# Transposes in one group: h of the last tile and x of the next behind the first eight products of an expert step

## The reference, cut to what matters

```python
def swiglu(x, w_gate, w_up, w_down):
    return (jax.nn.silu(x @ w_gate) * (x @ w_up)) @ w_down

    def run_block(args):            # one block: up to 128 tokens of one expert
        tok, gw, e = args
        return swiglu(x[tok], w1[e], w3[e], w2[e]).astype(F32) * gw[:, None]
...
    shared = swiglu(x, ws1, ws3, ws2).astype(F32)
    return (routed + shared).astype(h.dtype).reshape(B, T, D)
```

## Time and profile before

| | us |
|---|---|
| median of 3 executions | 2640.47 |
| lowest, highest | 2636.76, 2642.72 |
| profiled execution | 2637.47 |
| its span, first to last instruction | 2635.7 |

### The profile page before, as it was taken

How to read it: one execution, slowest core, us unless ns; L and a number is a source line. 1 busy time by engine, 2 the same in 40 slices (tenths; PEclk the granted TensorE clock), 3 DMA queues, 4 the chain that set the end, 5 groups by cost and what they waited for, 6 DMA issues and landing times. The chain is left out here.

```text
span 2635.7 us, 47416 instructions
## 1 busy us (share of the span) xinstructions
PE 2461.7 (93%) x11959; PEld 2011.9 (76%) x11960; DVE 1717.1 (65%) x2741; ACT 1012.1 (38%) x1619; POOL 988.2 (37%) x1009
## 2 busy tenths in 40 slices
PE   7999999998989999889999999999999999999990
PEld 4788777776767888668888887887888888888870
DVE  4663674557345666765567768587876768778673
ACT  2321433333432222222334445354554535445442
POOL 1211016542153677741233333333333433434344
PEclk8999999999989999989999999999999999999995
DMA  7775676756766556346869979899997989979887
GB/s 295 280 284 219 233 274 243 273 210 231 282 240 236 195 188 199 126 133 167 247 169 268 282 209 304 220 301 280 286 315 193 278 256 302 292 215 307 258 239 279
DMA packets 240999, 646.32 MB, mean 245 GB/s; under 512 B 24205, under 2 KB 37841, under 8 KB 224913
## 3 DMA queue, kind: packets, MB, share of 16 engines
q1 hardware_dynamic: 190480, 463.95, 49.1%
q0 software_dynamic: 50432, 181.27, 27.5%
HBM read 467.81 MB, written 177.33 MB: 245 GB/s over the span
## 5 line engine op out<-in xcount | busy, mean ns | idle before, releaser
L2429 PE MATMUL ps_h<-shared,x_exp_t_hi 128*128 (+1 forms) x2432 | 580.0, 391 | 7.4 <-ACT x_exp_t_hi L2196 7.4
L2429 PEld LDWEIGHTS ps_h<-shared,x_exp_t_hi 128*128 128x128 f32 x2432 | 457.2, 188 | 104.5 <-issue 9.1
L2145 POOL DMA_INDIRECT sum_d<-w_shared_raw,give x136 | 236.7, 1740 | 612.1 <-DMA sum_d<-w_shared_raw,give 276.5
L1216 PE MATMUL ps_p<-shared 128*128 128x512 f32 x1632 | 392.5, 399 | 6.5 <-DVE kvqg_out L105 3.3
L1216 PEld LDWEIGHTS ps_p<-shared 128*128 128x128 f32 x1632 | 308.5, 190 | 75.9 <-DVE kvqg_out L105 4.1
L2429 PE MATMUL ps_y<-shared,h_exp_t_hi 128*128 (+1 forms) x1216 | 342.4, 404 | 19.0 <-DVE h_exp_t_lo L2267 14.7
L2429 PE MATMUL ps_h<-shared,x_exp_t_lo 128*128 (+1 forms) x1216 | 318.6, 404 | 0.0
L2247 DVE TENSOR_TENSOR shared<-w_exp,shared (+1 forms) x256 | 307.0, 1220 | 10.0 <-ACT shared L2182 4.7
L2211 ACT ACTIVATE h_exp_t_hi<-ps_ht 128x256 fp32r<-128x256 f32 x152 | 58.4, 384 | 615.5 <-PE ps_ht L2438 613.3
L2429 PEld LDWEIGHTS ps_y<-shared,h_exp_t_hi 128*128 128x128 f32 x1216 | 220.1, 190 | 62.3 <-issue 22.0
L2182 ACT ACTIVATE shared<-w_exp (+1 forms) x256 | 255.4, 1056 | 22.5 <-DMA w_exp<-in_experts 19.5
(11 more groups left out here) (296 smaller groups left out, 3601.8 us busy)
## 6 DMA issues: line engine op xcount, KB each, us to landing
w_exp<-in_experts SPq DMA_DIRECT2D x386, 512.0 KB
shared<-hx_d SPq DMA_DIRECT2D x58, 1024.0 KB, 7.1
shared<-rec_d SPq DMA_DIRECT2D x16, 1536.0 KB
shared_raw<-in_w_mod_rest POOLq DMA_DIRECT2D x16, 1024.0 KB, 5.7
rec_d<-shared_raw SPq DMA_DIRECT2D x48, 256.0 KB, 5.0
rec_d<-kvqg_out SPq DMA_DIRECT2D x48, 256.0 KB, 4.6
hx_d<-shared SPq DMA_DIRECT2D x10, 1024.0 KB, 5.8
xt<-in_xt POOLq DMA_DIRECT2D x18, 512.0 KB, 8.3
```

Source lines behind the costliest of these rows:

```text
L1216: last = pe.matmul(ps_p[:, s % 2], hx0[:, at, x, k].bitcast(F32R), wa[w][:, k, p % 2 * HD:(p % 2 + 1) * HD].bitcast(F32R), start=(m + k == ...
L2145: pool.indirect_dma_start(sum_d[:, :], bass.IndirectOffsetOnAxis(give[:, par:par + 1], 0), y[:, par], None, compute_op=ALU.add).then_inc(a ...
L2429: last = pe.matmul(out, x[:, j * P:(j + 1) * P].bitcast(F32R), w_part[:, bass.ds(w_at + j * stride, 512)].bitcast(F32R), start=(start and ...
```

## The change

In the TensorE step the two transposes of h, which stood behind sixteen of the 24 h products, and the eight transposes of x, which stood behind all 24, are both put behind the first eight. The waits inside them move along. Nothing else is changed; the order of the products among themselves stays as it is.

```diff
                 products(ps_h[:, par], x_t[0][:, par], w[0], at, KC, 512, start=True)
+                if not isinstance(k, int) or k > 0:
+                    transposes_h(k - 1, 1 - par)
+                if not isinstance(k, int) or k >= NT - 1:
+                    transposes(k + 1, 1 - par, 0 if r is None else r + par)
                 pe.wait_ge(gu_lo, (e + 1) * N_GU)
                 products(ps_h[:, par], x_t[0][:, par], w[1], at, KC, 512)
-                if not isinstance(k, int) or k > 0:
-                    transposes_h(k - 1, 1 - par)
                 pe.wait_ge(xt_lo, (k + 1) * 2)
                 products(ps_h[:, par], x_t[1][:, par], w[0], at, KC, 512, stop=True).then_inc(h_done, 1)
-                if not isinstance(k, int) or k >= NT - 1:
-                    transposes(k + 1, 1 - par, 0 if r is None else r + par)
                 if not isinstance(k, int) or k > 0:
                     down(k - 1, 1 - par)
```

## The result

| | before | after |
|---|---|---|
| median, us (13 executions each, taken in turn) | 2641.20 | 2647.58 |
| lowest, highest | 2636.76, 2643.48 | 2639.95, 2652.60 |
| profiled execution | 2637.47 | 2649.45 |
| its span | 2635.7 | 2647.6 |

The ratio is 1.0024 with an interval of 1.0014 to 1.0033: slower by 6.4 us, where 2.1 us faster was forecast. The median of 2647.58 lies 1.6 us above the upper end of the range. The two profiled executions differ by 12.0 us, more than the medians do: that of before is 3.7 us under its median, that of after 1.9 us above its own.

The account below looks back on a forecast made before the run. TensorE was taken as the only full engine in the expert stage. The terms -5.2 + 1.6 + 1.3 + 0.2 = -2.1 us gave 2638.4 us on the median of 2640.47; the 8-in-10 range was 2632 to 2646.

Parts of the forecast that it names:

- The group's price: TensorE, each step: joining two transpose groups saves one entry and exit, 0.04 us, over 137 steps 5.2 us.
- The group costs nothing: Rival: TensorE's excess belongs to the transposes themselves, so 0 in place of -5.2, 2643.6 us; chance 0.12.
- x_exp_t_hi ... Cost 0.: Next step's first h product: x copies end 1.0 us ahead in place of 1.9, 0.6 us cover left; cost 0.
- TensorE starves at the step's start.: Rival: x_exp_t_hi's 1.0 us lead is too short, 0.1 to 0.2 us per step, about 2660 us; chance 0.06.
- Down products, +1.6 by a late H.: Weight changes: h products complete (H) later in the step, VectorE's run begins 0.27 us later at six places, 1.6 us.
- gain 0: Down product waits, 12 us: earlier h transposes take none away, as VectorE has no gap; gain 0, at most 12.
- Cover of H too thin: Rival: tile h 0.87 us later delays down products at six runs and eight steps, 2649 us; chance 0.10.
- The eight steps like the earlier trace: Steps where VectorE runs gapless to h_exp_t_lo: down products just fit, cost 0, or 0.3 us each, 2.4 us.
- The third gather.: First gather after the unrolled pair: x transposes want its tile earlier, TensorE stands 1.3 us, once (0 to 3.6).
- the waits that I put at 0 for ps_x and hg: Moved waits before the x and h transposes: x_exp_t_lo frees ps_x and hg is ready early enough; cost 0.
- The clock falls.: Rival: a run of ten transposes tips TensorE to half clock, 490 us more, 3130 us; chance 0.01.

Follow-up runs that it names:

- e3: Against before: only the h transposes move behind the first eight products, x transposes stay behind all 24; ratio 0.9994.
- e13: Against after: the joined group of ten transposes stands behind sixteen h products in place of eight; ratio to before 1.0029.
- e7: e5 with VectorE's low part of the h copy put ahead of its first two weight splits; ratio to before 1.0021.
- e12: e7 with only half of each weight piece loaded from the fourth expert on, so results are not the layer's; ratio to before 0.9927.
- e1: After, with ScalarE splitting the fourth gate/up weight piece one step earlier, together with the other three; ratio to before 1.0080.
- e2: Before, with the same ScalarE edit as e1 (fourth gate/up piece split one step earlier); ratio to before 1.0079.
- e5: After, with ScalarE's fourth gate/up split last in the step before, behind h copy and down splits; ratio to before 1.0020.

## Why the prediction was wrong

Going by its steps:

- **The group's price.** Right: 0.040 us per step predicted and measured. "The group costs nothing" falls.
- **"x_exp_t_hi ... Cost 0."** Here it failed. I followed the x copies to their end and took them for the last thing that the next start needs from ScalarE. Behind them, in the same queue, stands the fourth weight split, and where the expert ahead had a single tile the start needs that too. I read ScalarE from a quiet step, where it doesn't occur, and in the earlier trace rows, a change, only up to the tanh. The sum that I should have made: copies end at S + 7.4, a split of 1.0 behind them, so S + 8.4 before the change, 0.9 ahead of the next start at S + 9.33. 0.87 later it is at S + 9.2 to 9.3 with the next start due at S + 9.29, where an input has to be 0.4 ahead: 0.3 to 0.4 us late at each such change. Measured: 0.22, 28 times. All of it but the number of changes is in rows of before. That the first eight products behind a late input run 0.12 us slower is in no row that I had read.
- **"TensorE starves at the step's start."** This rival named the place but not the reason: it costs at 31 of 136 steps, not at each. The quiet steps show x_exp_t_hi 1.0 us ahead of S to be enough. Against the rival I had also brought the queue of 64 entries that the Trainium skill states (TensorE: Matmul & The Clock Gate, Engine queue depths), and had concluded from it that a late input matters less. The trace does not bear my conclusion out for an input that comes within 0.4 us of its product, as the row at 1450.75 shows; the queue itself no run here shows.
- **Down products, +1.6 by a late H.** Mechanism right, size too large. The waits lie in six pairs, each at a run of weight changes. Idle before the down products, in the order of time:

| | first of a pair | sum | second of a pair | sum |
|---|---|---|---|---|
| before | 0.85 0.85 0.69 0.89 0.89 0.63 | 4.8 | 1.53 2.25 0.86 0.86 0.83 0.88 | 7.2 |
| after | 0.90 0.92 0.89 0.89 0.89 0.92 | 5.4 | 0.93 1.96 1.31 1.76 1.55 2.39 | 9.9 |
| e3 | 0.50 0.51 0.81 0.54 0.51 0.51 | 3.4 | 1.93 2.10 1.25 0.83 2.15 0.84 | 9.1 |
| e13 | 0.84 0.82 0.87 0.94 0.91 0.98 | 5.4 | 0.87 0.90 1.00 0.86 0.84 1.61 | 6.1 |

The first of a pair is VectorE's, as I had read it. A later H makes it 0.1 us longer, in after and e13 alike: 0.6 us in place of 1.6. h transposes alone ahead (e3) make it 0.24 shorter, so my "gain 0" was not exact either, 1.4 us, which the second ones took back. The second is 0.85 at its least, and above 1 us it is another matter, that I had missed although 1.53 and 2.25 stood in the trace of before: ScalarE waits for a load. The largest but one in after, ScalarE, VectorE and TensorE:

```profile
1801.48 1.06 ACT L2182 ACTIVATE shared<-w_exp  x1 [1.70 <-DMA w_exp<-in_experts]
1802.90 1.07 ACT L2182 ACTIVATE shared<-w_exp  x1 [0.36 <-DMA w_exp<-in_experts]
1807.67 1.06 ACT L2182 ACTIVATE shared<-w_exp  x1 [3.71 <-DMA w_exp<-in_experts]
1808.64 0.37 ACT L2211 ACTIVATE h_exp_t_hi<-ps_ht 128x256 fp32r<-128x256 f32 x1
...
1805.69 2.35 DVE L2247 TENSOR_TENSOR shared<-w_exp,shared  x2
1809.04 0.42 DVE L2267 TENSOR_TENSOR h_exp_t_lo<-ps_ht,h_exp_t_hi 128x256 fp32r<-128x256 f32 x1 [0.99 <-issue]
...
1809.88 1.97 PE L2429 MATMUL ps_y<-shared,h_exp_t_hi 128*128 x4 [1.96 <-DVE h_exp_t_lo L2267]
```

The load lets the third split begin at 1807.67 only, the h copy of 0.37 us follows it, VectorE has been idle for 0.99 us by then, and TensorE stands for 1.96.
- **"Cover of H too thin"** gave 2649, near the measured time, for another reason: luck. The eight steps like the earlier trace rows did not turn into waits in the view, 12 before and 12 after. But they did not "just fit" either. In the kernel after, h_exp_t_lo ends at S + 6.16 in four of them and at S + 6.24 in the other four, where I had 6.09, and the down products follow it by 0.42. So they start on time or 0.09 late, and their first four take 1.02 us in place of 0.91: 1.3 us in all, in the rows "waits" and "first four" of the account. One of the eight, S = 2041.98, VectorE and TensorE:

```profile
2047.80 0.42 DVE L2267 TENSOR_TENSOR h_exp_t_lo<-ps_ht,h_exp_t_hi 128x256 fp32r<-128x256 f32 x1
...
2048.63 1.19 PE L2429 MATMUL ps_y<-shared,h_exp_t_hi 128*128 x4
2049.66 0.61 PE L2429 MATMUL ps_y<-shared,h_exp_t_lo 128*128 x2
```

- **The third gather.** 1.3 us predicted, 1.33 measured; the earlier trace rows have the same transposes without a wait. No other gather was late, and none of the waits that I put at 0 for ps_x and hg occurs. Timeline of TensorE in after:

```profile
1292.23 0.38 PE L2438 MATMUL ps_ht<-ident,shared_raw 128*128 128x128 f32 x2
1293.93 1.10 PE L2423 MATMUL ps_x<-ident,w_shared_raw 128*128 128x128 f32 x8 [1.33 <-DMA w_shared_raw<-h_d,take]
```

- **"The clock falls."** Not by the run of ten transposes: quiet steps keep 0.109 us per transpose and the stage 1.00, and the caution that I took from the Trainium skill's rule on transposes (the same page, Part 4) changed nothing. It fell for 3 us at one place, behind the wait above, where I had not looked for it. Windows of after, columns as above:

```profile
1810.00:1812.00 2.00, 2.00 (x5) 1.61 (x6) 1.50 (x4) 2.00 (x4) 1.23 (x2) 0.50 1.05 385
1812.00:1814.00 2.00, 2.00 (x7) 1.54 (x6) 1.87 (x4) 1.08 (x2) 0.72 (x2) 0.65 1.11 323
```

In numbers: the starts, +9.6 us, are the term that was missing, and -2.1 + 9.6 is +7.5 where the medians say +6.4. That this is so near is partly luck, as the account of the one profiled execution comes to +12.2.

**What stays open.** Whether the second waits of after, 2.7 us above those of before, and its place at half clock belong to the change or to this one execution. e13, whose H is as late, has 6.1 there, and its ratio is that of after; that speaks for the execution. So does that after's profiled execution lies 1.9 us above its median and before's 3.7 below. The account of e13 against before is -5.4 for the quiet steps, +9.8 in the starts, -1.2 in the waits and +2.3 in slower first down products, 5.5 us, and its loop is 5.7 us longer. That the loads themselves have no time to give is concluded from e7 and e12, and no kernel tried it with full loads.

## What to carry to other kernels

When work is put ahead of an instruction that others wait for, list all that is queued behind that release on each engine, in the rare kind of step (a weight change) before the common one, and follow each item to the next start. Read the waits of the weight loads along with those of the matmuls: a start that is a few tenths late shows there and in the distance of two starts, and nowhere else. Before a stall is repaired, see what is late next: here (e7) the time won in some 30 places was lost again in seven, where the loads come late and a long wait can cost half clock besides.

## What the runs showed that I had not expected

**A long wait costs TensorE more than its length.** Behind the longest waits before down products these mostly run at a granted clock of 0.50 (1.2 GHz) for some 3 us, in places twice that, which costs 1.1 to 2.2 us more: six places in e1 (waits of 2.99 to 3.77 us), five in e7 (2.67 to 3.85). One wait of 3.04 in e2 did not do it. Around 2 us it goes either way: 1.96 in after, 1.93 and 2.15 in e3 and 2.29 in e5 did it, 2.10 in e3, 2.25 in before and 2.39 in after did not. So the length of the wait alone does not say it.

**A late input costs twice.** The first product follows it by 0.40 us, and the eight that it opens take 1.94 us in place of 1.82. In after the same 0.11 to 0.12 us is lost on the first four down products behind a wait. In before it is not: there the x transposes stand right ahead of them, the four take 1.01 to 1.04 us in every step, and a wait adds nothing to that. With the joined group they take 0.91 in a quiet step, so a part of what the group saves is given back wherever their input is late, in some 20 places of after.

**One split ahead of a short copy.** Moving a split of 1.0 us in front of a copy of 0.4 cost 0.8% in both kernels (e1, e2), with the same loads: what counts is which short instruction stands behind a wait for memory.
